# Gates inside the cell, states in halves and sums by rows: a change to an mLSTM and sparse attention step

## The chip, the cores and the metric

The kernel runs on one core of one Trainium2 chip. Times are device microseconds (us) of one execution. PE is the tensor engine (PEld its weight loads), DVE the vector engine, ACT the scalar engine, POOL GpSimd, SP the engine whose queue issues most transfers; "PEq" and the like are the sequencers of the engines.

## The reference

One step of a two-layer model on one prompt of T = 512 tokens and S = 32 sample tokens (8 sequences of 4). Layer A is an mLSTM block (4 heads of 512), with a state C of 512x512, n of 512 and m for each of 8 sequences and 4 heads; layer B is attention over compressed, selected and window keys with caches. All is f32. Cut to what the change touches:

```python
xm, z = up[..., :A_INNER], up[..., A_INNER:]          # up = rmsnorm(x) @ w_up
xc = silu(conv4(xm));  conv_new = last 3 rows of xpad
q, k, v = headwise(xc, w_q), headwise(xc, w_k), headwise(xm, w_v)
gates = concat([q, k, v]) @ w_if + b_if;  ig = gates[:A_HEADS];  lf = log_sigmoid(gates[A_HEADS:])
b = cumsum(lf);  m_t = max(b + m_st, max_s(d));  d = causal(b_t - b_s + ig_s)
s = (q k^T) * exp(d - m_t);  w_inter = exp(b + m_st - m_t)
num = s @ v + w_inter * (q @ c_st);  den = sum(s) + w_inter * (q . n_st)
h = num / max(|den|, exp(-m_t))
c_new = decay * c_st + sum_s(w_row * k v^T);  n_new = decay * n_st + sum_s(w_row * k)
out = (headnorm(h) + skip * xc) * silu(z);  x = x + rmsnorm(out @ w_down)
kv = rmsnorm(x) @ w_kv                                # written out, and the window cache moved on
kcmp, vcmp = compress(rows of cached pages and of kv) # silu(flat @ w1 + b1) @ w2 + b2
```

## The kernel before

The kernel is a row of stages; each is a block, and all engines meet at its end (on POOL that end includes the landing of its transfers). In a block the order of each engine's work is written out by hand, and semaphores tie the engines. PSUM is used as a ring of 7 banks, filled by PE and drained by DVE or ACT; in the cell the ring has 6 and the bank `SUMS` is apart. f32 weight products of the projections are made as three products of halves, high by high, low by high and high by low (lines 405 to 407, 1188 to 1190, 1355 to 1357, 1739 to 1741): ACT copies the high part (`round_w`, `upper`), DVE subtracts to the low part (`rest_w`, `lower`), PE waits for `w_low`.

- **Up** (`stage_up`, up to 182.3 us): 16 features in two token halves. DVE convolves each (line 514), ACT makes its silu (line 488). At the end PE makes the gates' products, 32 columns of each feature, from xm (lines 418 and 420) and xc (line 426), half by half, in the banks `parts`, and folds them (`gate`, lines 437 and 438). It turns the last three rows of each sequence (`tails`, line 432); DVE copies them (line 556) and POOL stores them. POOL also adds xnT = high + low for a later stage.
- **Gates** (`stage_gates`, 182.3 to 197.2): |f|, softplus by ACT's Exp and Ln, two scans and the differences on DVE (lines 598 to 621), three exponentials on ACT, a turn of the rows on PE (line 586), and two small stores by SP.
- **Cell** (`stage_cell`, 197.2 to 540.3): four heads. `begin(h)` spreads the gates' rows by a product with `headsel` and makes k (line 743); v (765), turns, q, scores, then the prompt's state C (804) with key sums (805 and 807, one and eight columns, in `SUMS`), the numerators (826) with the denominators (827). Beside this go the 32 states of the samples, 1 MB each, in `cs`, a ring of `NCS` = 3 slots: SP loads (863) and stores (855) them, PE multiplies (715) and makes the update (722), DVE scales and adds (1012).
- **Gate** (`stage_gate`, from 540.3): z = xn w_up, with ACT's high parts of x and w, DVE's low parts (lines 1221 and 1224), then the product with silu(z).
- **Down**, then **kv** (`stage_kv`, 761.3 to 857.7): three chunks of 512 columns in 4 tiles and a sample tile; copies to `kvt` by ACT (line 1600), `fold` by DVE. POOL first copies the window caches from DRAM to DRAM (line 1571), and at the end stores the new window rows `o_wp` and `o_ws` (lines 1583 and 1585).
- **Compression** (`stage_compress`, from 857.7): 6 groups (kind s, pair c) of rows of 3 units. POOL puts a unit of cached pages side by side (`pair`), PE turns it (banks `R`), ACT and DVE split it into `Rh` and `Rl`; `posT` (line 1668) and `bias(s)` (1689) make the position's share; then the groups' products. Then queries and attention.

The wait for a ring slot of a state reads:

```python
for u in range(AH * SB):
    if u >= NCS:
        store_state(u - NCS)
        sp.wait_ge(k.c_stored[u % NCS], 16 * (u // NCS))
    sp.dma_start(cs[:, u % NCS, :, :], ...)
```

## Time and profile before

| | |
|---|---|
| median of 3 runs | 1578.62 us (1576.86 to 1579.74) |
| profiled execution | 1582.51 us, span 1580.6 |
| granted clock, mean | 0.942 |
| busy, share of the span | PE 90%, PEld 67%, DVE 45%, ACT 30%, POOL 12% |
| DMA | 182.08 MB, mean 115 GB/s |

Shares are means over stages with different limits. What a stage is worth is read from its own window and from the waits at its edges. A granted clock of 1.00 is the 2.4 GHz level, 0.50 the level of 1.2 GHz. Matmuls overlap: the duration of one is longer than the step from one start to the next.

### The profile page before, as it was taken

How to read it: one execution, taken by the hardware profiler on the slowest of the kernel's cores; microseconds unless marked ns; L12 is line 12 of the kernel's file. 1: busy time of each engine (PE TensorE's matmuls, PEld its weight loads, DVE VectorE, ACT ScalarE, POOL GpSimd, SP SyncE). 2: the span in 40 equal slices, each digit the busy share in tenths (PEclk: the TensorE clock that was granted, in tenths of full speed). 3: DMA queues.
4: the chain of work that ended last, by engine and by line, in shares of the span. 5: the costliest groups of instructions: out<-in, count | busy, mean ns of one | idle time of the engine just before them, and what ended most of it. 6: DMA issues, size and time to landing. Idle time of an engine off the chain costs nothing. (4 is left out here: it accounts for less than half of the span.)

```text
span 1580.6 us, 25096 instructions
## 1 busy us (share of the span) xinstructions
PE 1423.2 (90%) x9749; PEld 1054.9 (67%) x9749; DVE 708.7 (45%) x1413; ACT 481.2 (30%) x1125; POOL 190.3 (12%) x237
## 2 busy tenths in 40 slices
PE   5899399999997499998895999999999999999977
PEld 5899265656563299776674999888666555555555
DVE  4675424656654733616721332005033545455646
ACT  4232132333231322424421231121103333333433
POOL 4110240303030000000002210100000000010020
PEclk9899689999999699999897999996999999999988
DMA  6110025777778622232853323002131313141421
GB/s 179 54 54 1 6 87 186 234 231 224 237 228 255 245 98 107 70 107 105 285 178 104 98 81 120 1 17 97 54 118 28 103 40 116 49 108 55 114 74 57
DMA packets 92747, 182.08 MB, mean 115 GB/s; under 512 B 10023, under 2 KB 24003, under 8 KB 91427
## 3 DMA queue, kind: packets, MB, share of 16 engines
q1 hardware_dynamic: 89382, 163.76, 31.9%
q0 software_dynamic: 3248, 16.72, 3.2%
q8 instruction: 79, 1.29, 0.3%
q14 instruction: 38, 0.31, 0.1%
HBM read 133.82 MB, written 54.95 MB: 119 GB/s over the span
## 5 line engine op out<-in xcount | busy, mean ns | idle before, releaser
L1984 PE MATMUL ps<-xnT,wring 128*64 128x256 f32 (+1 forms) x1536 | 183.6, 397 | 1.3 <-PEq L2687 1.3
L1984 PEld LDWEIGHTS ps<-xnT,wring 128*64 128x64 f32 x1536 | 111.8, 138 | 64.1 <-issue 5.8
L1012 DVE SCALAR_TENSOR_TENSOR wring<-wring,nbw,ps 128x512 f32<-128x512 f32 x128 | 86.9, 740 | 69.0 <-PE ps L722 68.9
L2436 ACT ACTIVATE P<-ps,nmx 128x128 f32<-128x128 f32 (+3 forms) x128 | 66.3, 522 | 121.3 <-DVE nmx L2464 121.2
L1357 PE MATMUL ps<-wh,xl 128*128 128x512 f32 x224 | 89.2, 398 | 0.0
L405 PE MATMUL ps<-xuh,wuh 128*128 128x256 f32 (+1 forms) x256 | 78.9, 308 | 11.3 <-DVE wring_low L352 10.7
L2464 DVE TENSOR_REDUCE nmx<-ps 128x1 f32<-128x128 f32 (+3 forms) x128 | 56.8, 485 | 63.9 <-PE ps L2294 57.9
L1188 PE MATMUL ps<-xh,wh 128*128 128x256 f32 (+1 forms) x256 | 74.7, 292 | 10.2 <-DVE wl L1221 10.2
L406 PE MATMUL ps<-xul,wuh 128*128 128x256 f32 (+1 forms) x256 | 77.9, 304 | 0.0
L407 PE MATMUL ps<-xuh,wring_low 128*128 128x256 f32 (+1 forms) x256 | 77.6, 303 | 0.0
L1189 PE MATMUL ps<-xl,wh 128*128 128x256 f32 (+1 forms) x256 | 74.3, 290 | 0.0
L1190 PE MATMUL ps<-xh,wl 128*128 128x256 f32 (+1 forms) x256 | 73.8, 288 | 0.0
L804 PE MATMUL ps<-vt,kw 128*128 128x512 f32 x128 | 69.1, 630 | 0.0
L1739 PE MATMUL ps<-cRh,cwh 128*128 128x384 f32 x192 | 66.9, 348 | 0.0
L1741 PE MATMUL ps<-cRh,cwl 128*128 128x384 f32 x192 | 65.0, 339 | 0.0
L1740 PE MATMUL ps<-cRl,cwh 128*128 128x384 f32 x192 | 65.0, 338 | 0.0
L2290 PE MATMUL ps<-KT,Qp 64*128 64x128 f32 (+3 forms) x256 | 52.5, 485 | 12.2 <-ACT P L2436 12.2
L1310 DVE TENSOR_TENSOR wring_low<-wring,wh 128x512 fp32r<-128x512 f32 x64 | 40.9, 682 | 46.8 <-PE ps L1321 25.6
L1908 PE MATMUL ps<-xnT,wring 128*128 128x256 f32 (+1 forms) x256 | 58.9, 393 | 2.2 <-PEq L2902 2.2
L405 PEld LDWEIGHTS ps<-xuh,wuh 128*128 128x128 f32 x256 | 52.7, 206 | 11.7 <-issue 5.8
L2268 DVE COPY PT<-ps 128x128 f32<-128x128 f32 (+3 forms) x64 | 30.9, 483 | 66.1 <-PE ps L2358 65.4
L2578 POOL TENSOR_TENSOR arena<-arena,tmp 128x512 f32<-128x512 f32 x16 | 20.3, 1271 | 317.4 <-DVEq L2505 317.4
(475 smaller groups left out, 3078.2 us busy)
## 6 DMA issues: line engine op xcount, KB each, us to landing
wring<-in_state_C_dram SPq DMA_DIRECT2D x32, 1024.0 KB, 6.2
out_dram<-wring SPq DMA_DIRECT2D x32, 1024.0 KB, 8.3
wring<-in_a_w_up_dram SPq DMA_DIRECT2D x8, 2048.0 KB, 8.0
wring<-in_b_w_in_dram SPq DMA_DIRECT2D x8, 2048.0 KB, 9.6
wring<-in_a_w_down_dram SPq DMA_DIRECT2D x4, 2048.0 KB, 8.7
craw<-in_cache_kv_dram SPq DMA_DIRECT2D x64, 128.0 KB
arena<-in_cache_kv_dram SPq DMA_DIRECT2D x32, 256.0 KB, 3.9
arena<-in_cache_win_dram SPq DMA_DIRECT2D x8, 1024.0 KB, 5.9
```

Of the source, the lines that this page charges most:

```text
L405: pe.matmul(b[:, 0:t1 - t0], w_hi, x_hi, start=kt == 0, stop=False)
L406: pe.matmul(b[:, 0:t1 - t0], w_hi, x_lo, start=False, stop=False)
L407: m = pe.matmul(b[:, 0:t1 - t0], w_lo, x_hi, start=False, stop=kt == KD - 1)
L804: m = pe.matmul(b[:, :], keys, vt[:, j, :], start=j == 0, stop=j == NT - 1)
L1012: dve.scalar_tensor_tensor(out=c, in0=c, scalar=nbws[:, h % 2, 2 * S + s:2 * S + s + 1], in1=b[:, :], op0=ALU.mult, op1=ALU.add).then_inc( ...
L1188: pe.matmul(out, w_hi, x_hi, start=kt == 0, stop=False)
L1189: pe.matmul(out, w_hi, x_lo, start=False, stop=False)
L1190: m = pe.matmul(out, w_lo, x_hi, start=False, stop=kt == KD - 1)
L1357: m = pe.matmul(b, x_lo, w_hi, start=False, stop=last and kt == KD - 1)
L1739: pe.matmul(b[:, 0:CROW], w_hi, r_hi, start=j == 0, stop=False)
L1984: m = pe.matmul(b[64 * par:64 * par + 64, 0:t1 - t0], w[:, kt, x:x + DH], k.xnT[:, kt, t0:t1], start=kt == 0, stop=kt == KD - 1)
L2436: act.activation(P[:, n % 2, par, 0:w], b[:, 0:w], ACT.Exp, bias=nmx[:, n % 4, par:par + 1], accum_out=sm[:, i, h:h + 1]).then_inc(free, 1)
```

## The change

- **Up**: both halves' `parts` banks open together; the products of xm come first, then for each feature both halves of xc, with the tail turns before the last feature. ACT copies the tails instead of DVE. POOL issues the window caches' copies here (they leave the kv stage) and adds xnT in four rounds, and makes the first head's blocks.
- **Gates**: the stage is gone; its instructions are in the cell's programs, with rows in spare room of the ring and of new tile `late_rows`. PE turns them after head 0's queries, then `spread(0)`; later heads' `spread` comes before `begin`.
- **Sums**: key sums and denominators are made as 32 rows of 512 columns (`pick` or ones as weights), copied by ACT (`keep_rows`), turned (`turn_sums`), and summed by DVE.
- **States**: a slot is loaded and stored in two halves of 512 KB, and each load waits for the store issued one half earlier in the order than before.
- **Gate stage**: the first weights' high and low parts come before x, x in the order `XORDER`, three of eight low pieces on POOL, and PE takes both halves of the first block piece by piece.
- **kv and compression**: a class `PairRows` holds the work on the units. Units 0 to 2 (group 0) and `posT` are made in the kv stage, one unit after each chunk. The stores of `o_wp` and `o_ws` are issued by SP in the compression, ahead of unit 5. `bias(0)` stands first, `bias(1)` and the folds in group 0.

Moved code is not shown twice. The new names `part`, `held` and `load_half` are the half-slots' views and their load.

```diff
--- before.py
+++ after.py
...
+        parts_banks = [open_bank(pe, k, ("parts", hf)) for hf in range(2)]
...
+        for f in range(FT):
+            if f == FT - 1:
+                pe.wait_ge(k.tails_ready, 2)
+                for r in range(4):
...
+            pe.wait_ge(k.xc_ready, f + 1)
+            for hf in range(2):
+                m = gate_features(hf, f)
+                if f == FT - 1:
+                    m.then_inc(parts_banks[hf][1], 1)
...
+            for b in range(2 * r, 2 * r + 2):
+                pool.dma_start(k.o_ws[b, 0:512 - SI].rearrange("t a g d -> t (a g d)"),
+                               k.cache_win[b, SI:512].rearrange("t a g d -> t (a g d)")).then_inc(k.stored_win, 16)
+
+            for kt in range(2 * r, 2 * r + 2):
+                pool.tensor_tensor(k.xnT[:, kt, 0:T], k.xuh[:, kt, 0:T], k.xul[:, kt, 0:T], ALU.add)
+        drained(pool, k, ("bdt", 3, 2))
+        head_blocks(pool, k, 0)
...
+                act.activation(tails[:, :, 0:3], k.xp[:, :, T:T + 3], ACT.Copy).then_inc(k.tails_ready, 1)
+                act.activation(tails[:, :, 3:27].rearrange("p f (b j) -> p f b j", j=3), k.xs[:, :, :, 4:7], ACT.Copy).then_inc(k.tails_ready, 1)
...
+        for r in range(4):
+            b, free = full_bank(act, k, ("tail", r))
+            act.activation(tail_rows[:, 512 * r:512 * r + 512], b[0:27, :], ACT.Copy).then_inc(free, 1)
...
+        dve.tensor_copy(k.xms[:, :, :].rearrange("p f (b i) -> p f b i", i=SI), k.xs[:, :, :, 3:7])
...
-def stage_gates(nc, k, ctx):
...
+    cst = late_rows[:, 0:1024].rearrange("p (a e) -> p a e", a=2)
...
+    e, dif, b_sum, a_max = (late_rows[0:AH, TA * n:TA * n + TA] for n in range(4))
+    m_tok = late_rows[0:AH, 3072 - TA:3072]
+    gate_rows = k.wring[0:96, 1, 2048 + 2 * TA:2048 + 3 * TA]
+    ig, fg = k.gates[:, 0, :], k.gates[:, 1, :]
+    pick = sb("pick", [128, 32])
...
-            pe.wait_ge(k.c_here[u % NCS], 16 * (u // NCS + 1))
+            for half in range(2):
+                pe.wait_ge(k.c_here[2 * (u % NCS) + half], 16 * (u // NCS + 1))
...
+        def turn_sums(key):
+            sums, sums_full = open_at(pe, k, key, SUMS)
+            for ft in range(HF):
+                m = pe.transpose(sums[:, 128 * ft:128 * ft + 128], srow[:, 128 * ft:128 * ft + 128], k.ident[:, :])
+            m.then_inc(sums_full, 1)
...
+        def turn_gates():
+            pe.wait_ge(k.rows_ready, 1)
+            pe.wait_ge(k.wrow_ready, 3)
...
+        def spread(h):
...
+            if h == 0:
+                turn_gates()
+                spread(0)
...
+            for j in range(NT):
+                pe.matmul(sums[32 * j:32 * j + 32, :], pick[:, :], kw[:, j, :], start=True, stop=j > 0)
+            pe.matmul(sums[0:SB, :], k.tmask[0:S, :], kw[0:S, NT, :], start=False, stop=True).then_inc(sums_full, 1)
...
-                    keys = kw[:, j, 128 * ft:128 * ft + 128]
-                    m = pe.matmul(b[:, :], keys, vt[:, j, :], start=j == 0, stop=j == NT - 1)
-                    pe.matmul(sums[:, ft:ft + 1], keys, k.ones[:, 0:1], start=j == 0, stop=j == NT - 1)
+                    m = pe.matmul(b[:, :], kw[:, j, 128 * ft:128 * ft + 128], vt[:, j, :], start=j == 0, stop=j == NT - 1)
                 m.then_inc(full, 1)
-                n = pe.matmul(sums[:, HF + 8 * ft:HF + 8 * ft + 8], kw[0:S, NT, 128 * ft:128 * ft + 128], k.tmask[0:S, :],
-                              start=True, stop=True)
-            n.then_inc(sums_full, 1)
+            turn_sums(("nT", h))
...
+            sums, sums_full = open_at(pe, k, ("rows", h), SUMS)
+            for j in range(NT):
+                m = pe.matmul(sums[32 * j:32 * j + 32, :], k.ones[:, 0:32], P[:, j, :], start=True, stop=True)
+            m.then_inc(sums_full, 1)
             for i in range(NT):
+                if i == NT - 1:
+                    turn_sums(("den", h))
...
-                    n = pe.matmul(sums[:, i:i + 1], rows, k.ones[:, 0:1], start=j == 0, stop=j == i)
...
             if h + 1 < AH:
+                spread(h + 1)
...
+        for v in range(4):
+            load_half(v)
+        sp.wait_ge(k.rows_ready, 1)
+        sp.dma_start(k.o_mp[0, 0].unsqueeze(1), m_tok[:, T - 1:T]).then_inc(k.stored_m, 16)
...
+        for v in range(4, NH):
+            load_half(v)
+        store_half(0)
+        for v in range(NH, 2 * AH * SB):
+            store_half(v - NH + 1)
+            sp.wait_ge(k.c_stored[v % NH], 16 * (v // NH))
+            load_half(v)
...
+        def keep_rows(key):
+            b, free = full_bank(act, k, key)
+            act.wait_ge(k.stored_m, 32)
+            act.activation(srow[:, :], b[:, :], ACT.Copy).then_inc(free, 1)
...
+        act.wait_ge(k.absf_ready, 1)
+        act.activation(e[:, :], e[:, :], ACT.Exp, scale=-1.0).then_inc(k.softplus_ready, 1)
+        act.wait_ge(k.softplus_ready, 1)
+        act.activation(e[:, :], e[:, :], ACT.Ln, bias=1.0).then_inc(k.softplus_ready, 1)
...
+            if h == 0:
+                act.wait_ge(k.rows_ready, 1)
+                act.activation(k.brow[:, TA:TA + S + SB], k.brow[:, TA:TA + S + SB], ACT.Exp).then_inc(k.wrow_ready, 1)
+                act.activation(gate_rows[32:36, :], m_tok[:, :], ACT.Exp, scale=-1.0).then_inc(k.wrow_ready, 1)
+                act.activation(gate_rows[64:68, :], dif[:, :], ACT.Exp).then_inc(k.wrow_ready, 1)
...
+            keep_rows(("nn", h))
...
+            keep_rows(("rows", h))
...
+        dve.scalar_tensor_tensor(out=e[:, :], in0=fg, scalar=-1.0, in1=fg, op0=ALU.mult, op1=ALU.max).then_inc(k.absf_ready, 1)
...
+        dve.tensor_tensor(m_tok[:, :], b_sum[:, :], a_max[:, :], ALU.add).then_inc(k.rows_ready, 1)
+        b, free = full_bank(dve, k, "cols")
...
         begin(0)
+        drained(dve, k, "cols")
...
+            turned = b.rearrange("p (f j r) -> p f j r", f=HF, j=NT)
+            nn = turned[:, :, 0, 0:SB]
+            dve.reduce_sum(nP[:, HF * h:HF * h + HF], turned[:, :, :, SB], axis=AX.X)
...
+            st.then(dve.reduce_sum(rr[:, 1, :], b.rearrange("p (i j r) -> p i j r", i=NT, j=NT)[:, :, :, 0], axis=AX.X))
...
+    WS, XD = 5, 5
...
+    XORDER = [0, 5, 1, 2, 6, 3, 4, 7]
...
-                b, full = open_bank(pe, k, ("z", f, hf))
+            banks = []
+            for n in range(2 * KD):
+                hf, kt = (n % 2, n // 2) if f == 0 else (n // KD, n % KD)
+                t0, t1 = HALF[hf]
+                if kt == 0:
+                    banks.append(open_bank(pe, k, ("z", f, hf)))
+                if f == 0 and hf == 0:
+                    if kt < XD:
+                        pe.wait_ge(k.x_low, kt + 1)
+                    else:
+                        pe.wait_ge(k.x_rest, kt - XD + 1)
+                b, full = banks[hf]
...
+    @block.gpsimd
+    def _(pool):
+        for kt in range(XD, KD):
+            pool.wait_ge(k.x_high, XORDER.index(kt) + 1)
+            pool.tensor_tensor(xl[:, kt, :], k.xnT[:, kt, :], xh[:, kt, :], ALU.subtract).then_inc(k.x_rest, 1)
...
     def _(act):
         def upper(f):
             act.activation(wh[:, f % WS, :, :], weights(act, f), ACT.Copy).then_inc(k.w_high, 1)
-        for kt in range(KD):
+        upper(0)
+        for n in range(KD):
+            kt = XORDER[n]
             act.activation(xh[:, kt, :], k.xnT[:, kt, :], ACT.Copy).then_inc(k.x_high, 1)
...
+        lower(0)
+        for kt in range(XD):
+            dve.wait_ge(k.x_high, XORDER.index(kt) + 1)
             dve.tensor_tensor(xl[:, kt, :], k.xnT[:, kt, :], xh[:, kt, :], ALU.subtract).then_inc(k.x_low, 1)
...
+class PairRows:
...
+    def side(self, pool, u):
+        k = self.k
+        pool.wait_ge(k.raw_here[u % NRAW], 64 * (u // NRAW + 1))
+        if u >= 2:
+            bank, n = k.bank_of[("R", u - 2, 1)]
+            pool.wait_ge(k.bank_full[bank], n)
+        for a in range(2):
...
+    def turn(self, pe, n, a):
+        k, u = self.k, self.unit(n, a)
+        pe.wait_ge(k.pair_ready, u + 1)
...
+    def lower(self, dve, n, a):
+        k = self.k
+        for gp in range(2):
+            b, free = full_bank(dve, k, ("R", self.unit(n, a), gp))
+            dve.wait_ge(k.r_high, 2 * (3 * n + a) + gp + 1)
+            dve.tensor_tensor(self.half(k.Rl, n, a, gp), self.turned(b), self.half(k.Rh, n, a, gp), ALU.subtract).then_inc(free, 1)
...
-            between = [(16, lambda: samples(1)), (24, lambda: samples(2)), None][c]
+            between = [(16, lambda: samples(1)), (24, lambda: samples(2)), (16, lambda: pr.turn(pe, 0, 2))][c]
...
+            if c == 0:
+                pe.wait_ge(k.cw_here, 16 * 6)
+                b, full = open_bank(pe, k, "posT")
+                pe.transpose(b[:, 0:32], k.posr[:, :], k.ident[0:32, 0:32]).then_inc(full, 1)
+            if c < 2:
+                pr.turn(pe, 0, c)
...
-        for q in range(2):
+        for q in range(4):
+            if q >= NRAW:
+                sp.wait_ge(k.pair_ready, q - NRAW + 1)
             cached_rows(sp, k, 0, q)
...
-        for s in range(SB):
-            pool.dma_start(k.o_ws[s, 0:512 - SI].rearrange("t a g d -> t (a g d)"),
-                           k.cache_win[s, SI:512].rearrange("t a g d -> t (a g d)")).then_inc(k.stored_win, 16)
+        for u in range(2):
+            pr.side(pool, u)
...
-        pool.wait_ge(k.kv_here, 3 * (NT + 1))
-        pool.dma_start(k.o_wp[0].rearrange("(i p) s g d -> p i (s g d)", p=128), kvt[:, 0, 0:NT, :]).then_inc(k.stored_win, 16)
-        for s in range(SB):
-            pool.dma_start(k.o_ws[s, 512 - SI:512].rearrange("t a g d -> t (a g d)"),
-                           kvt[SI * s:SI * s + SI, 0, NT, :]).then_inc(k.stored_win, 16)
-        pool.wait_ge(k.stored_kv, 16 * 4)
+        pr.side(pool, 2)
...
+                if c == 2 and i == 2:
+                    pr.upper(act, 0, 2)
...
+            if c < 2:
+                pr.upper(act, 0, c)
...
+            if c == 0:
+                dve.wait_ge(k.pad_clear, 3)
+                b, free = full_bank(dve, k, "posT")
+                dve.tensor_copy(k.posT[:, 0:32], b[:, 0:32]).then_inc(free, 1)
+            pr.lower(dve, 0, c)
...
+        bias(0)
...
-                    turn(n + 1, (j - 2) // 5)
+                    pr.turn(pe, n + 1, (j - 2) // 5)
+                if n == 0 and j in (5, 14):
+                    fold_bias(j // 14)
+                if n == 0 and j == 10:
+                    bias(1)
...
             sp.wait_ge(k.pair_ready, u - NRAW + 1)
+            if u == 5:
+                sp.dma_start(k.o_wp[0].rearrange("(i p) s g d -> p i (s g d)", p=128), kvt[:, 0, 0:NT, :]).then_inc(k.stored_wp, 16)
+                for b in range(SB):
+                    sp.dma_start(k.o_ws[b, 512 - SI:512].rearrange("t a g d -> t (a g d)"),
+                                 kvt[SI * b:SI * b + SI, 0, NT, :]).then_inc(k.stored_wp, 16)
...
-        for p in range(1, 4):
+        for p in range(4):
             upper(0, p)
...
+        for u in range(3, 2 * NS):
+            pr.side(pool, u)
+        pool.wait_ge(k.stored_kv, 16 * 4)
+        pool.wait_ge(k.stored_win, 16 * SB)
...
+        for p in range(4):
             lower(0, p)
...
-            dve.tensor_tensor(pb[:, 2 * s:2 * s + 2], b[:, 0:2], k.vecs2[:, 24 + 2 * s:26 + 2 * s], ALU.add).then_inc(free, 1)
+            if p == 0:
```

## Rows read from the trace of the kernel before

**Rows 1.** Timeline of PE: the three largest waits (start us, us, engine, line, operation).
```profile
195.06 1.03 PE L586 MATMUL ps<-ident,rows 96*128 96x96 f32 x5 [22.29 <-ACT rows L635]
...
547.39 0.58 PE L1188 MATMUL ps<-xh,wh 128*128 128x256 f32 x1 [10.23 <-DVE wl L1221]
...
857.85 0.28 PE L1668 MATMUL ps<-ident,posr 32*128 32x32 f32 x1 [11.94 <-PEq L2899]
```
**Rows 2.** Windows: gates stage and cell; busy PE, PEld, DVE, ACT, POOL, clock, DMA.
```profile
182.30:197.20 14.90, 1.03 (x5) 0.69 (x5) 8.60 (x17) 6.70 (x8) 1.28 (x4) 0.50 0.00 0
197.20:540.30 343.10, 313.32 (x1514) 187.56 (x1514) 189.63 (x430) 104.49 (x207) 75.09 (x78) 0.96 0.66 217
```
**Rows 3.** Line 514 (ns: least, median, most), and the end of up by timeline.
```profile
L514 DVE SCALAR_TENSOR_TENSOR convt<-arena,vecs,convt x48: 808/810/1711, 50.7 to 160.1; 128x568 f32<-128x568 f32 x48
...
156.59 1.90 PE L426 MATMUL ps<-xcT,wc 128*32 128x256 f32 x30
...
169.83 1.93 PE L432 MATMUL ps<-ident,tails 128*27 128x128 f32 x16
...
174.84 2.47 DVE L556 COPY crow<-ps 27x512 f32<-27x512 f32 x4
...
182.34 0.54 POOL L592 MEMSET wring<- 4x544 f32 x1 [3.64 <-POOLq L2870]
```
**Rows 4.** Timelines of DVE, PE and ACT, from the gates to the states.
```profile
192.63 0.70 DVE L621 TENSOR_TENSOR m_tok<-b_sum,a_max 4x544 f32<-4x544 f32 x1
...
200.39 6.60 PE L743 MATMUL ps<-xcT,bd 128*128 128x256 f32 x16 [0.71 <-POOL bd L165]
...
212.78 0.59 ACT L949 ACTIVATE vt<-ps 32x512 f32<-32x512 f32 x1
...
226.53 1.12 PE L804 MATMUL ps<-vt,kw 128*128 128x512 f32 x2
```
**Rows 5.** Timeline of PE: products of the prompt's state, and their sums.
```profile
227.63 1.10 PE L804 MATMUL ps<-vt,kw 128*128 128x512 f32 x2
228.57 0.28 PE L805 MATMUL ps<-masks,kw 128*128 128x1 f32 x2
228.71 1.10 PE L804 MATMUL ps<-vt,kw 128*128 128x512 f32 x2
...
230.95 0.38 PE L807 MATMUL ps<-tmask,kw 32*128 32x8 f32 x2
...
232.23 1.06 PE L715 MATMUL ps<-wring,qm 128*32 128x512 f32 x8
```
**Rows 6.** Timelines of DVE, PE and SP's queue at the end of head 3.
```profile
478.12 2.72 DVE L1012 SCALAR_TENSOR_TENSOR wring<-wring,nbw,ps 128x512 f32<-128x512 f32 x4 [8.65 <-PE ps L722]
...
490.03 0.37 SPq L863 DMA_DIRECT2D wring<-in_state_C_dram  x1
...
498.97 0.37 SPq L863 DMA_DIRECT2D wring<-in_state_C_dram  x1
...
496.39 1.93 PE L715 MATMUL ps<-wring,qm 128*32 128x512 f32 x8 [7.37 <-DMA wring<-in_state_C_dram]
...
524.70 2.72 DVE L1012 SCALAR_TENSOR_TENSOR wring<-wring,nbw,ps 128x512 f32<-128x512 f32 x4 [3.15 <-PE ps L722]
```
**Rows 7.** Timeline of DVE at the start of the gate stage.
```profile
546.12 4.62 DVE L1221 TENSOR_TENSOR wl<-wring,wh 128x1024 fp32r<-128x1024 f32 x4
```
**Rows 8.** Timelines of ACT, DVE and PE, projection and start of compression.
```profile
789.47 2.74 ACT L1600 ACTIVATE arena<-ps 128x512 f32<-128x512 f32 x4 [15.55 <-PE ps L1357]
...
846.61 1.13 DVE L1622 COPY V<-arena 128x256 f32<-128x256 f32 x5
...
875.07 0.41 PE L1739 MATMUL ps<-cRh,cwh 128*128 128x384 f32 x1
```
**Rows 9.** DMA issues of the page: each one's KB, median us to landing.
```profile
out_dram<-wring SPq DMA_DIRECT2D x32, 1024.0 KB, 8.3
...
out_dram<-cst POOLq DMA_DIRECT2D x16, 256.0 KB, 4.8
```

More of the change, by code:

```diff
@@ L744, in turned_products @@
                               start=True, stop=True).then_inc(full, 1)
-        def begin(h):
+        def turn_sums(key):
[6 more added lines that the diff above has]
+            pe.wait_ge(k.wrow_ready, 3)
+            b, full = open_bank(pe, k, "cols")
+            for i in range(NT + 1):
+                n = 128 if i < NT else S
+                m = pe.transpose(b[0:n, 96 * i:96 * i + 96], gate_rows[:, 128 * i:128 * i + n], k.ident[0:96, 0:96])
+            m.then_inc(full, 1)
+        def spread(h):
             b, full = open_bank(pe, k, ("nm", h))
@@ L1637, in stage_compress @@
     prow = free[:, 4 * CROW + 2048:4 * CROW + 2560].rearrange("p (s n) -> p s n", s=2)
-    posT = free[:, 4 * CROW + 2560:4 * CROW + 2624]
-    pb = free[:, 4 * CROW + 2624:4 * CROW + 2628]
-    groups = [(s, c) for s in range(2) for c in range(3)]
+    pb = free[:, 4 * CROW + 2560:4 * CROW + 2564]
+    kvt = k.arena[:, 0:(NT + 1) * D].rearrange("p (c i x) -> p c i x", c=2, i=NT + 1)
+    groups = GROUPS
+    pr = PairRows(k, pair)
     NG = len(groups)
@@ L1713, in output, with fold_bias @@
                     m.then_inc(full, 1)
-        for a in range(3):
-            turn(0, a)
-        bias(0)
-        bias(1)
-        for s in range(2):
+        def fold_bias(s):
             b, full = open_bank(pe, k, ("pb", s))
@@ L1771, in upper @@
             act.activation(wh[:, p, :, :], w[:, 4 * p:4 * p + 4, :], ACT.Copy).then_inc(k.w_high, 1)
-        def upper_rows(n, a):
-            for gp in range(2):
-                b, _ = full_bank(act, k, ("R", unit(n, a), gp))
-                act.activation(half(Rh, n, a, gp), turned(b), ACT.Copy).then_inc(k.r_high, 1)
-        upper(0, 0)
-        for a in range(3):
-            upper_rows(0, a)
-        for p in range(1, 4):
+        for p in range(4):
             upper(0, p)
@@ L1827, in lower, with keep_pos, keep_bias @@
             dve.tensor_tensor(wl[:, p, :, :], w[:, 4 * p:4 * p + 4, :], wh[:, p, :, :], ALU.subtract).then_inc(k.w_low, 1)
-        def lower_rows(n, a):
-            for gp in range(2):
-                b, free = full_bank(dve, k, ("R", unit(n, a), gp))
-                dve.wait_ge(k.r_high, 2 * (3 * n + a) + gp + 1)
-                dve.tensor_tensor(half(Rl, n, a, gp), turned(b), half(Rh, n, a, gp), ALU.subtract).then_inc(free, 1)
+        def keep_pos(s):
+            b, free = full_bank(dve, k, ("pos", s))
+            dve.tensor_copy(prow[:, s, :], b[:, 0:256]).then_inc(free, 1)
+        def keep_bias(s):
+            b, free = full_bank(dve, k, ("pb", s))
+            dve.tensor_tensor(pb[:, 2 * s:2 * s + 2], b[:, 0:2], k.vecs2[:, 24 + 2 * s:26 + 2 * s], ALU.add).then_inc(free, 1)
         def keep_output(n):
@@ L1883, in _ @@
                         lower(1, a - 1)
[L1884 removed]
+                    pr.lower(dve, n + 1, a)
+                    if n == 0 and a == 1:
+                        keep_pos(1)
+                if n == 0:
+                    keep_bias(1)
                 if (s, c) == (0, 2):
@@ L2898, in build @@
             k.posr = sb("posr", [32, 128], where=ahead)
+            k.posT = sb("posT", [128, 64], where=ahead)
+            k.Rh, k.Rl = [sb("cRh0", [128, 8, CPL], F32R, where=ahead)], [sb("cRl0", [128, 8, CPL], F32R, where=ahead)]
             with ExitStack() as c:
```

346 lines of the change are left out of this document (140 added, 206 removed).

## The prediction, made before the changed kernel was timed

> **What bounds the kernel now.** I read the chain of waits of TensorE (PE) first, then the stage windows, then the timeline at each large wait. PE is busy 90% of the span, so time can leave in two ways: its idle stretches close, or it issues less. The largest waits stand at stage boundaries: 22.3 us for the gate rows, 11.9 us at the start of the compression stage, 10.2 us at the start of the gate stage [rows 1]. The gates stage is 14.9 us with 1.03 us of PE work, at a granted clock of 0.50, which is the 1.2 GHz level, after PE had gone idle; the cell that follows is 343.1 us with 313.3 us of PE work [rows 2]. So four places count: tail of up plus gates, the cell's own PE work, the cell's last head, and projection to compression. The profiled run took 1582.5 us around a span of 1580.6; the median of the runs is 1578.6, so what comes out for the profiled run is lowered by 3.9 us.
>
> **Tail of up, and gates inside the cell.** Today the last convolution runs to 161.8, PE then makes the second half's products and the tail transposes to 171.8, DVE copies the tail rows to 177.3, POOL issues their stores, and 3.64 us after its last one the next stage opens at 182.34 [rows 3]. After: the row products of both halves and features 0 to 14 fill PE's wait. From 155.7 PE has about 1.0 us of first-half rows, 3.1 of second-half rows, 3.9 of features (62 instructions at the 63 ns of the 30 in 1.90 us) and 1.93 of transposes: it ends at 165.6 [rows 3]. It is the later one: with POOL's additions moved away, the convolution's steps fall from 1.71 us back to 0.81 (both in one row), and it ends near 158.6. ScalarE (ACT) copies the tail rows by 165.9, POOL issues 1.1 us of stores, plus 3.6, so the cell opens at 170.6. DVE's four gate additions (2.0 us, after 0.9 of copies and 1.0 of folds) end by 168.7, under that store.
>
> The first key product starts at 170.7 instead of 200.39 [rows 4]. The gate chain, which took 182.34 to 193.33 on DVE, now lies beside keys and values. It adds waits. ACT makes Exp and Ln before it empties a key bank, 4.1 us, which the six free banks cover. ACT then waits, ahead of the queries' copies, for `rows_ready`: due at 181.7, while ACT finishes the values at 183.7 (13.0 us after the first key product, as today) [rows 4], so that wait is free; the three exponentials (2.8 us with the table) hold the query banks, and PE, with six of eight banks filled, stands about 2 us. Then `turn_gates` and `spread(0)` add 1.8 us that stood before the stage. Cp of head 0 starts 26.1 us after the first key product today [rows 4], 30.6 after: at 201.3 instead of 226.53. **Gain 25.2.** If that cover is gone, up to 11.0 us (the whole chain) come back; I take 4.5 lost in it.
>
> POOL now adds xnT and issues the window copies during up. The row of rows 3 shows DVE doubled while POOL adds, eight additions of 1.5 us; DVE has room there except at 50 to 75 us, where it catches up. Between 0 and 5.9 us; I take 1.5, since most pieces meet a DVE with slack. **Loss 1.5.** The Trainium skill (GPSIMD Engine Reference, Specifications) says the SBUF interface is shared and contended by DVE instructions with two SBUF inputs. The trace agrees with 1.71 against 0.81 us.
>
> **Sums by rows.** One full f32 product and its one-column companion take 1.08 us from start to start; the companion's share is 0.23 us, since the product alone is two passes of 0.43. L807 costs 0.31 [rows 5]. Removed per head: 16 + 10 companions (6.0) and four L807 (1.25), 7.25 us. Added: four 32-wide products that run side by side, as the eight instructions of L715 in 1.06 us [rows 5], twice, so 2.1; one 32-row product 1.0; two times four transposes 0.5 each. That is 4.1. ACT's two copies of 0.6 us and DVE's reductions lie where both have slack. Net 3.15 a head. **Gain 12.6** for four heads. If the four do not run side by side (0.85 each), 5.1 a head more is added: the bound above is a loss of 7.8.
>
> **States in halves.** Near the end of head 3 the ring is the limit: state 25 was updated by 480.8, but the load that replaces it was issued at 490.03, the next at 498.97, because each load waits for a store that was issued 0.5 us after the previous load. PE stood 7.4 us [rows 6]. In halves a load waits for a store one turn older, with another store in flight, so backlog goes. The replaced slot then goes store (4 to 5 us) and load (5 us) after DVE: about 3.5 us of PE's wait remain, 3.9 go, and with them 1.3 us that L715 and L722 lost at the 0.50 clock after it. At the very end DVE sat 3.15 us for the last state [rows 6] and now runs through, being the bound: 3.05. **Gain 8.2**; ends: 0 (period unchanged) and 14 (all waits of this head gone).
>
> By the Trainium skill (DMA: Bandwidth & Descriptors, Bandwidth) transfers should be at least 1 MiB: 6.15 us for 1 MB and 79.0 for 16 MB make, as an estimate, 3.7 us for a half, 1.2 us more per MB if nothing overlaps. The period of 8.9 would be 11.3 and the total about 7 us slower than today. No row of this case has a 512 KB transfer under that load.
>
> **Gate stage.** Weights of the first block first and three of eight pieces on POOL: PE starts after one weight copy, one difference (4.62/4) and one x piece, 4.0 us after the stage opens instead of 7.05 [rows 1, 7]. **Gain 3.0** (0 if the chunk lands late: it is issued only once all stores have landed; 5 at best).
>
> **Projection.** In chunk 0 the copies of the pages are taken in before DVE's next weights. ACT starts its four copies at 789.47 and ends at 792.2 [rows 8], then splits two banks (1.2), DVE follows, then the first weight difference: PE resumes at 794.9 instead of 791.5, 3.4, and 1.0 for a low clock. Chunk 1: 1.5. Chunk 2: the turn, 1.0. **Loss 6.9**, ends 3.3 (the turns alone) and 11.
>
> **Compression.** DVE ends the projection at 847.7, but POOL has nine stores to issue, and their landing opens the stage at 857.7; the first group's products then start at 875.07 [rows 1, 8]. After, nothing of POOL is outstanding: the stage opens at 848.1; ACT's weight copy (1.06) and DVE's difference (1.7) give 851.2. That is 23.9 earlier; the second bias product (2.3, half of L1689's 4.7), folds (1.0) and 1.35 us of low clock move into the group. The nine stores now go through SP ahead of unit 5's pages: about 4.5 us of issue; unit 5 is then ready 17.7 us into the stage, its turn is due at 21.9. **Gain 19.2**, ends 12 and 22. What is late next there is `w_low` of the first block.
>
> **Sum.** 25.2 - 1.5 + 12.6 + 8.2 + 3.0 - 6.9 + 19.2 = 59.8. 1582.5 - 59.8 = 1522.7 for a profiled run, 1518.8 for the median.
>
> **Rivals.** *The new waits cost more.* The gate chain is late (up to 6.5 us more), DVE's order in the projection costs 4 more, the compression gains 5 less: 1534. For it: each chain crosses three engines; against: each has a slack that I counted. *The ring stays as it is.* Halves don't overlap better and the waits of head 3 remain: 1518.8 + 8.2 = 1527. *More closes than counted.* States, gate stage and projection at their good ends (5.8, 2, 3.6): 1507. *Slower, by the ring.* A store of 256 KB takes 4.8 us and one of 1 MB 8.3 [rows 9], so one of 512 KB about 6.0; if halves land one behind another, a state takes 11.9 us. From the first store (236.6 today, 211.4 after) the last load is issued 29 states later: at 556.5 instead of 516.56, and only 15.3 us of gain stand behind the cell: 1578.6 + 40 - 15.3 = 1603. It decides from 11.05 us a state, where the total is today's; today's 8.9 and two halves in flight speak against it. *That the change does not do what it says*: a wait on the stores of the maxima or a bank would keep the gates serial; then 11.0 us come back: 1530, inside the first rival.
>
> **Chances.** Forecast (1511 to 1527) 0.50; costlier waits 0.20; ring unchanged 0.12; more closes 0.12; slower by the ring 0.02; anything else 0.04, of which 0.02 slower. A measurement of this kernel can tell about 0.2% (3 us) from no change. Faster 0.95, same 0.01, slower 0.04. The range from 1502 to 1540 takes in all but the last two.
>
> **What would show it.** Right: the gate chain's DVE rows lie beside key and value products and Cp of head 0 starts near 201; heads 1 and 2 are 3 us shorter each; the period of a state's loads falls under 8 us; the first group of the compression starts 3 us after its stage opens; waits between chunks of the projection grow. Wrong: a wait of PE of over 5 us between queries and scores of head 0, a load period above 9, PE waiting for the low weights over 5 us between chunks 0 and 1, or an up stage whose products wait for DVE longer than today.

## The result and the profile after

The changed kernel took 1539.53 us (1538.08 to 1541.95, 4 runs), the kernel before 1577.74 beside it: a ratio of 0.9762, interval 0.9739 to 0.9785. That is 38.2 us faster, where 59.8 were forecast. The profiled execution of the changed kernel took 1538.08, 44.4 less than the profiled one of before. The 6 us between the two differences are the spread of single executions: the one of before lay 4.8 over its median, that of the changed kernel 1.4 under. The comparison below is of the two profiled executions, so its sum is 44.2 us of span.

The page of the changed kernel says which engine the time left. PE issues 136 instructions less and is busy for 15.0 us less; the other 29 us are idle stretches of PE that closed. Of the 15.0 us, 8.6 lie in the gates and the cell, where the 136 instructions went. In up, and in projection and compression together, PE makes as many instructions as before (1155 and 1317) in 2.5 and 3.6 us less busy time: there they ran at a higher granted clock (0.93 after 0.90 in up, 1.00 after 0.95 in the compression).

```profile
span 1536.4 us, 24936 instructions
PE 1408.2 (92%) x9613; PEld 1025.1 (67%) x9613; DVE 715.0 (47%) x1415; ACT 487.3 (32%) x1139; POOL 183.8 (12%) x231
```

The stages by windows, columns as in [rows 2]. First the kernel before: up, gate stage with down, projection, compression, the rest (gates and cell are in [rows 2]).

```profile
0.00:182.30 182.30, 144.02 (x1155) 138.69 (x1155) 102.59 (x144) 55.15 (x123) 43.05 (x61) 0.90 0.21 64
...
540.30:761.30 221.00, 202.40 (x1256) 178.65 (x1256) 98.89 (x157) 83.34 (x152) 0.00 (x0) 0.95 0.30 106
761.30:857.70 96.40, 80.19 (x356) 59.82 (x356) 32.44 (x60) 23.96 (x45) 11.45 (x22) 0.89 0.59 200
857.70:1002.80 145.10, 138.73 (x961) 131.71 (x961) 40.70 (x64) 35.57 (x57) 23.03 (x36) 0.95 0.28 88
1002.80:1580.60 577.80, 543.56 (x4502) 357.82 (x4502) 235.86 (x541) 171.96 (x534) 36.42 (x37) 0.96 0.23 70
```

Then the changed kernel: up, cell with the gates in it, gate stage with down, projection, compression, the rest.

```profile
0.00:170.95 170.95, 141.47 (x1155) 136.02 (x1155) 104.48 (x138) 57.93 (x130) 48.81 (x73) 0.93 0.35 117
170.95:506.10 335.15, 305.77 (x1383) 164.30 (x1383) 200.59 (x456) 115.27 (x223) 73.41 (x79) 0.95 0.67 223
506.10:724.70 218.60, 202.54 (x1256) 177.97 (x1256) 100.28 (x154) 83.11 (x153) 5.52 (x3) 0.96 0.30 105
724.70:825.00 100.30, 83.53 (x381) 62.47 (x381) 36.28 (x68) 27.20 (x50) 8.01 (x10) 0.92 0.30 95
825.00:958.10 133.10, 131.79 (x936) 126.55 (x936) 35.51 (x58) 31.94 (x51) 17.58 (x30) 1.00 0.34 106
958.10:1536.40 578.30, 543.09 (x4503) 357.81 (x4502) 237.80 (x541) 171.86 (x534) 30.44 (x37) 0.96 0.23 70
```

Up and the gates together went from 197.20 to 170.95 (26.3 less), the cell from 343.1 to 335.2 although the gates' chain is now in it, the compression from 145.1 to 133.1. The projection is the one stage that grew, by 3.9, although it no longer ends with the landing of the window stores. It now holds 25 PE instructions that stood in the compression before. The last line shows that nothing was given back behind: 577.8 and 578.3.

PE's timeline of the changed kernel gives the places. Each bracket is a wait; the lines without one mark where Cp, the prompt's state, of heads 0, 1 and 3 starts. (A count is of the instructions inside the window that was asked for: the row at 430.56 is the same as the two above it, cut by its window.)

```profile
171.13 5.59 PE L683 MATMUL ps<-xcT,bd 128*128 128x256 f32 x16 [4.46 <-PEq L2957]
...
186.55 1.18 PE L683 MATMUL ps<-xcT,bd 128*128 128x256 f32 x4 [2.32 <-ACT qT L925]
...
205.75 3.70 PE L766 MATMUL ps<-vt,kw 128*128 128x512 f32 x8
...
280.42 3.70 PE L766 MATMUL ps<-vt,kw 128*128 128x512 f32 x8
...
430.56 1.98 PE L766 MATMUL ps<-vt,kw 128*128 128x512 f32 x4
...
459.98 1.93 PE L655 MATMUL ps<-wring,late_rows 128*32 128x512 f32 x8 [4.42 <-DMA wring<-in_state_C_dram]
...
487.69 1.93 PE L655 MATMUL ps<-wring,late_rows 128*32 128x512 f32 x8 [3.90 <-DMA wring<-in_state_C_dram]
...
509.23 0.55 PE L1227 MATMUL ps<-xh,wh 128*128 128x256 f32 x1 [6.33 <-DVE xl L1273]
...
796.22 0.79 PE L1404 MATMUL ps<-wh,xh 128*128 128x512 f32 x1 [10.79 <-DVE arena L1422]
...
825.18 1.07 PE L1780 MATMUL ps<-wring,posT 128*32 128x256 f32 x16 [2.23 <-PEq L2986]
```

Against [rows 1]: the wait of 22.3 for the gates' rows has become 4.46 at the stage and 2.32 among the queries; 11.9 at the compression has become 2.23; 10.2 at the gate stage 6.33. New is one line: **10.79 us before chunk 2 of the projection, released by DVE's line 1422**, the last addition of a fold. In the kernel before PE waited 2.53 us there, for its first low weight:

```profile
820.10 0.66 PE L1355 MATMUL ps<-wh,xh 128*128 128x512 f32 x1 [2.53 <-DVE wring_low L1310]
```

### The profile page after: what moved, and what is told of

Same layout as the page of the kernel before. It is cut to its first block and busy times, and to the rows that moved or that the text cites. A ratio compares the mean times of both kernels' runs of the same rounds, so it can differ in the third digit from the quotient of the medians.

```text
span 1536.4 us, 24936 instructions
## 1 busy us (share of the span) xinstructions
PE 1408.2 (92%) x9613; PEld 1025.1 (67%) x9613; DVE 715.0 (47%) x1415; ACT 487.3 (32%) x1139; POOL 183.8 (12%) x231
## 5 line engine op out<-in xcount | busy, mean ns | idle before, releaser
L405 PE MATMUL ps<-xuh,wuh 128*128 128x256 f32 (+1 forms) x256 | 79.1, 309 | 11.5 <-DVE wring_low L352 10.8
L1616 DVE TENSOR_TENSOR cRl<-ps,cRh 128x512 fp32r<-128x512 f32 x36 | 23.2, 686 | 94.9 <-ACT cRh L1609 94.9
L405 PEld LDWEIGHTS ps<-xuh,wuh 128*128 128x128 f32 x256 | 52.5, 205 | 11.9 <-issue 5.9
```

Of the source, the lines that this page charges most:

```text
L405: pe.matmul(b[:, 0:t1 - t0], w_hi, x_hi, start=kt == 0, stop=False)
```

## The experiments

All are the changed kernel with one edit, but for the second, which adds to the first, and the last two, which put several together. Windows are taken from a landmark ahead of the edit to one behind it, since the same stages ahead of an edit lie up to 3.3 us apart between executions. How much a window itself varies is read from the other kernels, whose edits don't touch it.

**The projection: fold first.** Whose wait are the 10.79 us?

```diff
             hv.rest_w(dve, CH_KV + c, None if c else 0)
-            if c == 2:
-                dve.wait_ge(k.kvt_free, 1)
-            fold(dve, k, st, ("kv", c), kvt[0:S, c % 2, NT, :])
+            if c < 2:
+                fold(dve, k, st, ("kv", c), kvt[0:S, c % 2, NT, :])
+            if c == 1:
+                dve.wait_ge(k.kvt_free, 1)
+                fold(dve, k, st, ("kv", 2), kvt[0:S, 0, NT, :])
```

> DVE folds the samples' sums of chunk 2 in chunk 1, before it takes the low parts of unit 1; its low weights stay where they are. Theory (bank): the 10.8 us that PE waits before chunk 2 is the ring of 7 banks: two banks more per chunk put chunk 2's first tile on the bank of the samples' sums, which DVE folds only after eight low weights. Then PE waits for the first low weight only, as before the change: 3.9 us, and the kernel is 7 us faster than the changed one. Rival (order): DVE is simply too late with its weights, after the unit's low parts and the copies to KT and V; then the fold's place changes nothing, 0 us.

```profile
789.69 0.64 PE L1404 MATMUL ps<-wh,xh 128*128 128x512 f32 x1 [3.91 <-DVE wring_low L1359]
```

The wait is 3.91 us, and its releaser is now the first low weight. The expectation that the bank held PE stands: in the changed kernel that weight was ready at about 789.2, yet PE went on only at 796.2, when DVE had made eight low weights (from 788.52) and the fold. Counted in the code: from the bank of the samples' sums of chunk 2 to chunk 2's first tile there are six openings (tile 3 of chunk 1, two of unit 1, three of the turned keys), so the tile is the seventh and meets the same bank. Before, without the unit's two, it was tile 2, 11 us later. The kernel took 1534.83 (1532.14 to 1535.96), 4.7 less than the changed one. From the first product of chunk 1 to that of chunk 2 it is 32.0 us against 38.9, so 6.9 in the window. In five other executions that don't touch it this stretch took 37.3 to 37.4 us, and the compression then opened about 1.0 us later behind chunk 2, so the bank is worth about 6 to 7.

**The low weights too.** The edit is shown against the run above.

```diff
         for c in range(3):
-            hv.rest_w(dve, CH_KV + c, None if c else 0)
             if c < 2:
+                hv.rest_w(dve, CH_KV + c, None if c else 0)
                 fold(dve, k, st, ("kv", c), kvt[0:S, c % 2, NT, :])
             if c == 1:
+                hv.rest_w(dve, CH_KV + 2)
                 dve.wait_ge(k.kvt_free, 1)
                 fold(dve, k, st, ("kv", 2), kvt[0:S, 0, NT, :])
```

> As fold_early, and the low weights of chunk 2 are made ahead of unit 1's low parts as well, in DVE's idle stretch. Theory (bank first, weights second): PE does not wait before chunk 2 at all, 10.8 us and about 1 us of low clock less than the changed kernel. Rival (order alone): the same 11 to 12 us, so this run tells only together with fold_early. Rival (the sums' products of chunk 2 are late too, so DVE cannot do it earlier): under 3 us.

DVE's timeline of this kernel: the low weights are begun after 12.12 idle us, where DVE in the changed kernel stands idle for 20.88, and PE waits 0.19 us before chunk 2.

```profile
776.17 4.91 DVE L1359 TENSOR_TENSOR wring_low<-wring,wh 128x512 fp32r<-128x512 f32 x8 [12.12 <-PE ps L1370]
781.11 0.68 DVE L1420 COPY arena<-ps 32x512 f32<-32x512 f32 x1
```

1526.68 us (1524.33 to 1528.00), 12.9 less than the changed kernel, where 11.8 were expected. So most of the projection's loss was an order on DVE, not the turns' own work on PE.

**The last half state.**

```diff
-            store_half(v - NH + 1)
+            if v < 2 * AH * SB - 1:
+                store_half(v - NH + 1)
             sp.wait_ge(k.c_stored[v % NH], 16 * (v // NH))
             load_half(v)
+        store_half(2 * AH * SB - NH)
```

> The last half state is loaded before, not after, the store that stands ahead of it in SP's queue; its own slot's store is long issued. Theory (queue): that load was issued at 482.57 only because the store before it waited for DVE's update of state 29, behind the head's norm; now it is issued near 474, PE's wait of 3.9 us and DVE's of 4.4 us for the last state go: 4.4 us faster than the changed kernel. Rival (transfer): the halves' landing bounds it, then under 1 us.

Here `v` counts half states and `NH` = 6 half slots. SP's queue and DVE in the changed kernel show what the edit is about. The load at 482.57 is the last half. It stands behind the store at 482.14, which had to wait for DVE's update of state 29, behind the head's norm.

```profile
470.24 0.38 SPq L824 DMA_DIRECT2D wring<-in_state_C_dram  x1
482.14 0.37 SPq L830 DMA_DIRECT2D out_dram<-wring  x1
482.57 0.46 SPq L824 DMA_DIRECT2D wring<-in_state_C_dram  x1
...
480.64 5.35 DVE L1011 SCALAR_TENSOR_TENSOR wring<-wring,nbw,ps 128x512 f32<-128x512 f32 x8
```

With the edit that load is issued by 473, PE's wait for the last state is gone from its timeline, and DVE makes the last three updates with one gap of 0.38 us. From the first key product to the first product of the gate stage it is 334.5 us against 338.1: 3.6 us. In four other executions that leave this stretch alone it took 337.8 to 338.3. The timed runs say the same: 1535.96 (1535.69 to 1538.16). Expected were 4.4.

**The stores of the window rows.** POOL issues them at the end of the projection.

```diff
+        pool.wait_ge(k.kv_here, 3 * (NT + 1))
+        pool.dma_start(k.o_wp[0]..., kvt[:, 0, 0:NT, :]).then_inc(k.stored_wp, 16)
+        for b in range(SB):
+            pool.dma_start(k.o_ws[b, 512 - SI:512]..., ...).then_inc(k.stored_wp, 16)
...
-            if u == 5:
-                (the same nine on SP)
```

> The nine stores of the window rows are issued by POOL at the end of the projection again, all else as in the changed kernel. Theory: the compression opens only after their issue (4.9 us) and landing (about 3.6 us), 7 to 9 us later than now, of which nothing is hidden: 7 to 9 us slower than the changed kernel. Rival: what brought the compression its 21.6 us is only that the first group's rows are ready ahead; then 0 to 2 us.

```profile
822.00 4.25 POOL L1700 DMA_DIRECT2D out_dram<-arena  x8
...
833.69 1.17 POOL L1583 COPY arena<-craw 128x512 f32<-128x512 f32 x2 [7.43 <-POOLq L2986]
...
833.80 2.79 PE L1785 MATMUL ps<-wring,posT 128*32 128x256 f32 x24 [11.91 <-PEq L2986]
```

PE waits 11.91 us at the stage's opening instead of 2.23. The kernel takes 1549.15 (1548.33 to 1551.93), 9.6 more, a little over the 7 to 9 expected. Of the 21.7 us that the compression gained, 9.7 are issue and landing of the stores, which no longer stand between the stages. The other 12.0 are put down to the first group's rows and bias by subtraction; no run takes these back, and part of it is the granted clock of the stage, 1.00 after 0.95.

**The gates' cover.**

```diff
+        pe.wait_ge(k.rows_ready, 1)
         begin(0)
         for h in range(AH):
```

> As the changed kernel, but PE waits for the gates' rows before head 0's keys, as if the chain on DVE and ACT had no cover. Theory: the first key product moves from 171.1 to 182.0 (the chain's last row), 10.9 us, of which the 2.3 us wait among head 0's queries comes back: 8.6 us slower than the changed kernel. Rival (the chain is late for the head anyway): under 3 us.

```profile
182.44 3.89 PE L683 MATMUL ps<-xcT,bd 128*128 128x256 f32 x8 [15.33 <-DVE late_rows L1074]
```

The first key product starts 11.3 us later, Cp of head 0 11.4, and the span is 11.0 longer; the timed runs say 13.6 (1553.14, 1549.08 to 1555.33). Expected were 8.6. The 2.32 us among the queries did not come back: they are ACT's three exponentials and their table, which stand behind the values here too (194.64 to 197.5), though the rows were there at 182.

**The sums.** PE's companions of one and eight columns are back (the removed lines of the diff), with DVE's reads of them; `keep_rows` and the turns are gone.

```diff
-                    m = pe.matmul(b[:, :], kw[:, j, 128 * ft:128 * ft + 128], vt[:, j, :], ...)
+                    keys = kw[:, j, 128 * ft:128 * ft + 128]
+                    m = pe.matmul(b[:, :], keys, vt[:, j, :], ...)
+                    pe.matmul(sums[:, ft:ft + 1], keys, k.ones[:, 0:1], ...)
...
-            turn_sums(("nT", h))
```

> Key sums and denominators by one-column and eight-column companions again, all else as changed. Theory: head to head 77.7 us instead of 75.0, 2.7 us a head; of head 3's share some is hidden, since its states wait anyway: 9 to 11 us slower than the changed kernel. Rival (the heads got shorter for another reason, the earlier spread or the halves): head to head under 76, under 4 us.

The first companions of heads 0 and 1:

```profile
204.72 0.28 PE L765 MATMUL ps<-masks,kw 128*128 128x1 f32 x2
...
282.22 0.28 PE L765 MATMUL ps<-masks,kw 128*128 128x1 f32 x2
```

Head to head that is 77.5 us (78.0 and 78.0 for the next two), against 74.7 in the changed kernel (205.75 to 280.42), then 75.1 and 75.1. That is 2.9 a head. From the first key product to the gate stage it is 348.9 us against 338.1, 10.8 more, inside the 9 to 11 expected. The timed runs give 12.8 more (1552.36, 1551.65 to 1555.86).

**The states whole.** One load and one store of 1 MB a state, in the order of the kernel before, with the two stores of the maxima where they are now.

```diff
-        for v in range(NH, 2 * AH * SB):
-            store_half(v - NH + 1)
-            sp.wait_ge(k.c_stored[v % NH], 16 * (v // NH))
-            load_half(v)
+        for u in range(NCS, AH * SB):
+            store_state(u - NCS)
+            sp.wait_ge(k.c_stored[u % NCS], 16 * (u // NCS))
+            load_state(u)
...
```

> States loaded and stored whole again, in the order of the kernel before, all else as changed. Theory (ring): the ring turns in 9 to 10 us and must serve a head of 75 us in 9.4 us a state, so it falls behind: PE waits 5 to 12 us more in head 3 than the 4.4 us of the changed kernel, and the kernel is 5 to 12 us slower. Rival (halves bring nothing, since head 3 gained only 0.6 us in all): within 2 us of the changed kernel.

```profile
459.39 1.93 PE L654 MATMUL ps<-wring,late_rows 128*32 128x512 f32 x8 [4.53 <-DMA wring<-in_state_C_dram]
...
468.09 1.94 PE L654 MATMUL ps<-wring,late_rows 128*32 128x512 f32 x8 [4.82 <-DMA wring<-in_state_C_dram]
```

PE waits 10.8 us for states in head 3 instead of 8.3 (these two and 1.44 for the last one), and from the first key product to the gate stage it is 341.0 us instead of 338.1. That is 2.9 us for the halves, between the two expectations. The timed runs say 5.8 more, inside the first one's 5 to 12, but their ranges touch (1539.29 to 1547.07 against 1538.08 to 1541.95), so I take 3 and leave up to 6 open. The reason that was given did not hold: whole states did not fall behind in heads 0 to 2, where PE never waits for one.

**POOL's share in the gate stage.**

```diff
-    WS, XD = 5, 5
+    WS, XD = 5, 8
```

> All eight low pieces of x in the gate stage by DVE, none by POOL. Theory (contention): DVE's pieces took 1.35 us beside POOL's and 0.65 alone in the kernel before; alone again, eight of them end after 5.2 us instead of 6.7, the first block's half takes 7.4 instead of 9.0 us, and the kernel is 1.6 us faster than the changed one. Rival (POOL's pieces help): the eighth piece comes later than now and the kernel is 1 to 2 us slower.

DVE and POOL in the changed kernel, then DVE in this one:

```profile
508.36 6.74 DVE L1273 TENSOR_TENSOR xl<-xnT,xh 128x544 fp32r<-128x544 f32 x5
...
508.36 5.52 POOL L1243 TENSOR_TENSOR xl<-xnT,xh 128x544 fp32r<-128x544 f32 x3 [8.74 <-ACT xh L1252]
```

```profile
508.77 5.40 DVE L1273 TENSOR_TENSOR xl<-xnT,xh 128x544 fp32r<-128x544 f32 x8
```

DVE needs 1.35 us a piece beside POOL and 0.67 alone: eight alone are done sooner than five with help. The first feature's 48 instructions take 7.3 us instead of 9.0, the stage's products 97.7 instead of 99.5. The timed difference, 2.2 us, lies inside the runs' ranges (1537.33, 1535.18 to 1540.29); the window carries the claim. In the next two kernels, which have the same edit, the products take 98.8 and 98.1, so it is worth 0.7 to 1.7 us.

**Together.** The edits of the low weights, the last load and POOL's share in one kernel:

> low_early, last_load and gate_dve together. The three lie in different stages, so by theory they add: 1539.5 - 12.8 - 3.6 - 1.6 = 1521.5 us. Rival (some of it is given back downstream, by the first products of a stage at a low clock): 1524 to 1527.

1516.16 us (1515.35 to 1521.75), ratio to the kernel before 0.9625 (0.9606 to 0.9644), 23.4 less than the changed kernel; 18.0 were expected. The profiled executions differ by 21.6 us, of which 1.8 lie in up and 1.5 behind the compression, where nothing was edited: without these it is 18.3 us, which is what was expected. It beats both kernels. Then state 28 is moved behind two groups of numerators:

```diff
-                sample_state(pe, h, 3, 5)
+                sample_state(pe, h, 3, 4)
...
             for i in range(NT):
+                if i == 2 and late == SB:
+                    sample_state(pe, h, 4, 5)
```

and `new_states` on DVE likewise.

> best3, and in head 3 the fifth state (28) goes after two of the four groups of numerators instead of ahead of them, on PE and DVE. Theory: the 4.4 to 5.6 us that PE waits there for the state's second half is covered by products which are ready, and about 1 us of low clock behind it goes: 5 us faster than best3. Rival (the ring sets the end of the head: the later update holds back the last load): under 2 us.

```profile
460.18 1.06 PE L655 MATMUL ps<-wring,late_rows 128*32 128x512 f32 x8 [1.15 <-DMA wring<-in_state_C_dram]
```

The wait is 1.15 instead of 4.6, and the cell is 327.5 us long from key product to gate stage, against 333.7: 6.1 less. Yet the time, 1514.79 (1512.67 to 1516.38), is only 1.4 lower, inside the ranges of both. In the profiled executions up is 1.5 us longer with the move, and what follows the compression 3.1. The windows show the latter: first 20 us of the queries, then all that follows, in the kernel without the move and in the one with it.

```profile
938.00:958.00 20.00, 17.79 (x79) 14.93 (x79) 2.58 (x5) 3.65 (x16) 4.44 (x18) 1.00 0.00 1
938.00:1514.80 576.80, 541.92 (x4503) 357.34 (x4502) 235.88 (x541) 171.85 (x534) 36.43 (x37) 0.96 0.23 70
```

```profile
933.10:953.10 20.00, 17.79 (x72) 14.61 (x72) 2.57 (x5) 3.66 (x16) 4.44 (x18) 0.91 0.00 1
933.10:1513.00 579.90, 545.32 (x4503) 359.10 (x4502) 236.10 (x541) 171.97 (x534) 36.45 (x37) 0.96 0.23 70
```

The same 4503 instructions take 576.8 and 579.9 us; where the second lost is in part at a granted clock of 0.91 in its first 20 us, against 1.00. Over all profiled executions this stretch took 576.8 to 582.0 us, with no edit in it. Whether the moved state is worth more than 1.4 us over many runs stays open.

## Why the prediction missed

The direction and most steps held; the size did not: 38.2 us came where 59.8 were forecast. Applied to the 1578.62 us that stood ahead of the prediction, the ratio gives 1541.0: beyond the likeliest case (1511 to 1527) and just outside the range, which ended at 1540 (the bare median, 1539.53, is just inside). Two terms were mis-sized, both for a wait that was not followed to its end: the states at the end of head 3, and DVE's order in the projection. Together they make 14.4 of the 15.6 us by which the sum below is short. By the forecast's own steps, in the profiled executions:

| step | forecast | measured |
|---|---|---|
| up and gates, with contention | 23.7 | 22.8 |
| sums | 12.6 | 10.9 |
| states and end of head 3 | 8.2 | 0.5 |
| gate stage | 3.0 | 2.4 |
| projection | -6.9 | -13.6 |
| compression | 19.2 | 21.7 |
| the rest | 0 | -0.5 |
| sum | 59.8 | 44.2 |

How they were measured: Cp of head 0 starts 20.8 us earlier (226.53 in [rows 4], 205.75 now), and 2.0 of the sums' products now stand ahead of it. The sums are 2.7 us from head to head, taken four times, though only three such steps can be measured. The states are the 9.2 us gained from Cp of head 3 to the first product of the gate stage, less 4.7 of sums and 4.0 of the stage's opening. The gate stage is those 4.0 less 1.6 in its first feature. Projection and compression are cut where PE ends its projection work: 845.9 before, 822.9 after. In head 3 the split between sums and states is one of bookkeeping: undone one at a time in the changed kernel, the sums are worth 10.8 us and the halves 2.9.

**Up and gates: the steps held, one cost was left out.** The cell opens at 170.95, forecast 170.6; the convolution ends at 158.7, forecast 158.6; the rows are ready at 182.0, forecast 181.7; the wait among the queries is 2.32, forecast about 2. The contention in up cost nothing that can be seen: from first to last up product it is 128.9 us before and 128.8 after. The cover is real and worth 11 us (the run in which PE waits for the rows). But from the first key product to Cp of head 0 it is 34.6 us, of which 2.0 are sums: 6.5 more than the 26.1 of before, where 4.5 were forecast (the two terms given for them, 2 and 1.8, make 3.8). Behind the wait among the queries PE runs on at the 1.2 GHz level, which the forecast had not counted here:

```profile
189.87:194.19 4.32, 4.32 (x22) 4.07 (x21) 4.09 (x11) 2.13 (x7) 3.48 (x4) 0.50 0.19 73
```

These are the turns of the keys; in the kernel before they took 2.19 us at a granted clock of 1.00. That the row of the table is only 0.9 off is luck: the 1.5 us for contention were not spent, and made up for most of it.

**Sums: right mechanism, 1.7 us over.** The products side by side went as counted (eight instructions in 1.1 us); a head gained 2.7 instead of 3.15, and undoing it costs 2.9 a head. (The bound for products that don't run side by side was a little off: eight of 0.85 us instead of 2.1 make 4.7 a head more, not 5.1. It was not needed.)

**States: the first step that failed, 7.7 us.** I wrote that near the end DVE "now runs through, being the bound: 3.05", and that 3.9 of the 7.4 us would go. Of the first wait 2.95 went (7.37 in [rows 6], 4.42 now). The last state's wait did not go at all, 3.85 before and 3.90 now, and DVE sits 4.40 us there. Even the 2.95 did not last: from the end of the first wait to the first product of the gate stage it is 49.3 us against 51.0, although the stage's opening alone gained 4.0 of it. Of the 2.2 us lost there, 1.3 lie between PE's product at 479.03 (514.59 before) and its first one on the last state: 8.7 us against 7.4. I had followed each half's own chain, store then load, and had not asked what stands ahead of the load *in SP's queue*: a store one half newer, for a state that DVE updates only after the head's norm. Moving that one load gave 3.6 us. The rest of the miss lies about the first wait: the last kernel, which covers it with products that are ready, shortened the cell by 6.1 us. The low clock behind the first wait did not go either: the eight products of L655, which is L715 of the kernel before, still take 1.93 us.

**Projection: the second step that failed, 6.7 us.** Chunk 0 lost 2.6 us where 4.4 were forecast, and chunk 2 lost 0.9 of 1.0. Chunk 1, from its first product to that of chunk 2, went from 28.8 to 38.9: 10.2 us, where I had priced DVE's order at 1.5 and counted engines only. The wait was in the PSUM ring: two more banks between two points put a tile on a bank that is emptied last. The two runs of the projection show 6 to 7 us for the bank and all of the wait with the weights moved too. My sign of being wrong looked at the wrong pair: between chunks 0 and 1 PE waited 2.45 us for the low weights. The first rival had "DVE's order in the projection costs 4 more", the right place with a bit over half of what was missing. That its sum, 1534, was nearest of the cases is partly luck: the compression did not gain 5 less, and the states, which it left alone, were the larger miss.

**Gate stage.** The opening gained 4.0 instead of 3.0, and 1.6 were lost again since POOL's pieces double DVE's. The row in [rows 3] had shown that doubling (1.71 against 0.81), and I applied it to up, where nothing came of it, and not here, where it did.

**Compression: right, 2.5 us under.** The stage opened 2.1 us after PE's last product, as counted, and issue and landing of the stores alone are 9.7. The stage ran at a granted clock of 1.00 after 0.95; no run separates what of the 2.5 is that.

**Slower by the ring: no.** Halves turn at 6.4 us a state when nothing else holds them (five loads of halves from 457.4 to 470.2 us, 3.2 us apart). The estimate from the Trainium skill (DMA: Bandwidth & Descriptors, Bandwidth), that halves are 1.2 us worse per MB and the kernel some 7 us slower, did not come true here: whole states are 3 us slower. Presumably two halves under way at once overlap what one of 1 MB pays alone; no run separates that.

## What to carry to other kernels

When work is put between two points of an engine that fills banks in rotation, count the openings between them: two more banks can put the next product on a bank that another engine empties last, and the price is then what stands in that engine's queue, not the added work. When a transfer is split to start earlier, read the queue in its order and ask of the transfer just ahead whom it waits for. And read an element-wise helper on POOL at its price to DVE first: here three pieces taken over cost more than they saved, since DVE's own took twice as long on average.

## What the hardware showed that was not expected

- Eight subtractions of 128x544 on DVE alone took 5.40 us; five took 6.74 with POOL making three beside them (5.52). The doubling is a mean: of the five, two took 0.72 us, as alone, and three 1.88, one for each of POOL's. If the two engines take turns, the 3.4 us by which the five are late are POOL's three pieces, 1.1 each, as an estimate, where an addition of 128x512 on POOL took 1.27 in up. The Trainium skill (SBUF — State Buffer, Terms) says that the port pair of DVE and GpSimd is exclusive and held for a whole instruction; this trace fits that, within those 0.2 us a piece.
- Half the bytes are not half the time. The page's medians from issue to landing, for the changed kernel and then for the one with whole states, are 5.1 against 6.1 us for a load and 5.3 against 8.2 for a store:

```profile
wring<-in_state_C_dram SPq DMA_DIRECT2D x64, 512.0 KB, 5.1
out_dram<-wring SPq DMA_DIRECT2D x64, 512.0 KB, 5.3
```

```profile
wring<-in_state_C_dram SPq DMA_DIRECT2D x32, 1024.0 KB, 6.1
out_dram<-wring SPq DMA_DIRECT2D x32, 1024.0 KB, 8.2
```

- The same last stretch took 576.8 to 582.0 us in executions whose instructions in it are the same. It is the size of the smaller gains here, so these were read from windows.
